# A transformer pair on one core: seven products for eight in half of the steps of four more turns, with the gt2 loads among them

## The reference

```
mod = silu(c) @ w_ada + b_ada                # 6 x 2048: sh1, sc1, gt1, sh2, sc2, gt2
...attention of the first block; x = x + gt1 * mix
h2  = rms_norm(x, g_norm2) * (1 + sc2) + sh2
ffn = (silu(h2 @ w_gate) * (h2 @ w_up)) @ w_down      # 2048 -> 5632 -> 2048
x   = x + gt2 * ffn
...second block: convolution, forgetting attention, gates, relu^2 feed-forward 2048 -> 8192 -> 2048
```

## Time and profile before

| | us |
|---|---|
| median of three runs | 2602.41 (2600.86 to 2602.66) |
| the profiled execution | 2601.97 |
| its span, first to last instruction | 2600.2 |
| TensorE busy | 2550.3 (98%) |
| VectorE busy | 1781.0 (68%) |
| ScalarE busy | 1258.8 (48%) |
| GpSimd busy | 55.2 (2%) |
| granted TensorE clock, mean | 0.995 |

### The profile page before, as it was taken

One profiled execution on the slowest core, in us unless ns is written; L12 is line 12 of the kernel. 1 busy time (PEld: TensorE's weight loads), 2 busy tenths in 40 slices (PEclk: granted clock), 3 DMA queues, 4 the chain that ended last, 5 costly groups with the idle time before them and its releaser, 6 DMA issues.

```text
span 2600.2 us, 31671 instructions
## 1 busy us (share of the span) xinstructions
PE 2550.3 (98%) x11970; PEld 2048.5 (79%) x11970; DVE 1781.0 (68%) x2059; ACT 1258.8 (48%) x1647; POOL 55.2 (2%) x88
## 2 busy tenths in 40 slices
PE   7999989999999999999999999999999999999998
PEld 3677757788888888888888888888888888888886
DVE  2356664767779998978655455556689778777855
ACT  2344554443444555544544455444456555455544
POOL 1010110000000000000000000000000000000000
PEclk9999999999999999999999999999999999999999
DMA  9968776757776555565655545656655565556563
GB/s 392 400 229 304 260 273 224 260 199 244 248 246 217 202 203 199 194 215 190 212 194 178 178 162 167 206 200 211 200 177 198 189 221 192 186 188 220 190 196 121
DMA packets 263722, 564.34 MB, mean 217 GB/s; under 512 B 9315, under 2 KB 13589, under 8 KB 262445
## 3 DMA queue, kind: packets, MB, share of 16 engines
q1 hardware_dynamic: 261264, 549.25, 61.1%
q0 software_dynamic: 1952, 11.27, 1.2%
q10 hardware_dynamic: 380, 2.13, 0.2%
HBM read 558.40 MB, written 4.21 MB: 216 GB/s over the span
## 4 chain that ended last, share of the span: by engine, by line
PE 84%; DVE 2%; ACT 1%; issue 0%; POOL 0%; DVEq 0%; ACTq 0%; POOLq 0%
PE acc L528 59%; PE acc L885 15%; PE bank L885 3%; PE bank L611 2%; PE acc L923 1%; PE bank L560 1%; DVE w_lo L1998 1%; PE acc L848 0%; PE acc L761 0%; PE acc L813 0%; PE bank L770 0%; PE acc L759 0%; PE bank L623 0%; PE acc L1071 0%; PE acc L1072 0%
## 5 line engine op out<-in xcount | busy, mean ns | idle before, releaser
L1998 DVE TENSOR_TENSOR w_lo<-raw,w_hi 128x1024 fp32r<-128x1024 f32 x852 | 1008.3, 1193 | 582.6 <-ACT w_hi L1375 552.1
L1375 ACT ACTIVATE w_hi<-raw 128x1024 fp32r<-128x1024 f32 x804 | 845.7, 1059 | 761.4 <-PE acc L528 581.8
L528 PE MATMUL acc<-w_hi,actT_hi 128*128 128x512 f32 (+1 forms) x1344 | 531.4, 395 | 2.6 <-DVE actT_lo L2149 1.6
L528 PE MATMUL acc<-w_hi,actT_lo 128*128 128x512 f32 (+1 forms) x1344 | 521.3, 388 | 0.0
L528 PE MATMUL acc<-w_lo,actT_hi 128*128 128x512 f32 (+1 forms) x1344 | 520.9, 388 | 0.0
L528 PE MATMUL acc<-w_hi,mixT_hi 128*128 128x512 f32 (+1 forms) x1256 | 494.9, 394 | 2.5 <-DVE mixT_lo L2138 2.1
L528 PE MATMUL acc<-w_hi,mixT_lo 128*128 128x512 f32 (+1 forms) x1256 | 488.5, 389 | 0.0
L528 PE MATMUL acc<-w_lo,mixT_hi 128*128 128x512 f32 (+1 forms) x1256 | 487.8, 388 | 0.0
L528 PEld LDWEIGHTS acc<-w_hi,actT_hi 128*128 128x128 f32 x1344 | 252.4, 188 | 78.1 <-issue 19.1
L528 PEld LDWEIGHTS acc<-w_hi,actT_lo 128*128 128x128 f32 x1344 | 252.3, 188 | 52.3
L528 PEld LDWEIGHTS acc<-w_lo,actT_hi 128*128 128x128 f32 x1344 | 252.6, 188 | 50.0 <-issue 1.1
(11 more groups left out here) (357 smaller groups left out, 2000.9 us busy)
## 6 DMA issues: line engine op xcount, KB each, us to landing
raw<-in_w_ff SPq DMA_DIRECT2D x128, 1024.0 KB, 5.2
raw<-in_w_in SPq DMA_DIRECT2D x108, 1024.0 KB, 5.1
raw<-in_w_ada SPq DMA_DIRECT2D x64, 1024.0 KB, 6.4
raw<-in_w_gate SPq DMA_DIRECT2D x44, 1024.0 KB, 5.1
raw<-in_w_up SPq DMA_DIRECT2D x44, 1024.0 KB, 5.7
raw<-in_w_down SPq DMA_DIRECT2D x44, 1024.0 KB, 5.2
early_mix<-in_w_ada SPq DMA_DIRECT2D x16, 1024.0 KB, 10.5
wide<-in_w_ada SPq DMA_DIRECT2D x16, 1024.0 KB, 8.7
```

Source lines behind the costliest of these rows:

```text
L528: last_mm = pe.matmul(acc[p][:, t, 0:width], act[x][:, k0 + c, t * P:(t + 1) * P], w[:, u % SPL, c * NW:c * NW + width], start=first and c ...
L1375: act.activation(w_hi[:, u % SPL, :], raw[:, ld % RAW, slot[2] * 1024:(slot[2] + 1) * 1024], ACT.Copy).then_inc(hi_ready, 1)
L1998: dve.tensor_tensor(w_lo[:, u % SPL, 0:n], src, w_hi[:, u % SPL, 0:n].bitcast(F32), ALU.subtract).then_inc(lo_ready, 1)
```

## The change

Two of the four steps of gate and up in turns 1 to 4 become seven-product steps; the other two stay as units. The four "a" loads of a turn are placed one load sooner (after the first to the fourth weight load instead of after the second to the fifth), so that they lie ahead of the pairs. VectorE's gt2 products move with them: the first of a turn falls into the last down group of the turn before, and for the first turn into the first gate and up block. The activation differences are written in that same block, after units 7, 9, 11 and 13. `wide` is cleared by GpSimd behind its load of the gt2 bias, and VectorE waits for that before its first hidden product. Three of the four turns are a loop on TensorE, ScalarE and VectorE; SP's loads of these turns are written out.

```diff
-ORDER += "w" * 8 + ("w" + "wa" * 4 + "w" * 7) * 4 + "w" * 12 * 6 + "w" * 4
+ORDER += "w" * 8 + ("wa" * 4 + "w" * 8) * 4 + "w" * 12 * 6 + "w" * 4
...
-S_LOADS = [len(GAPS) + 8 + 4 * 12 + 12 * t for t in range(S_TURNS)]
+F1_LOAD = len(GAPS) + 8
+S_LOADS = [F1_LOAD + 12 * t + 4 for t in range(4)]
+S_LOADS += [F1_LOAD + 4 * 12 + 12 * t for t in range(S_TURNS)]
...
-        for _ in range(S_STEPS):
+        for _ in range(S_STEPS if w >= F1_LOAD + 4 * 12 else S_STEPS // 2):
             slots_ += [("pair", w, 1, w + 1), ("sums", 1), ("sums", 0), ("quarter", w + 1, 3), ("half", w + 1, 0),
                        ("half", w, 0)]
+            events += [DU * w, DU * w + 1, DU * w + 2, DU * w + 3, None, None]
...
@@ TensorE
-            def strassen(mixes):
+            def strassen(mixes, plain=0):
...
+                def ends(ins):
+
+                    ins.then_inc(unit_used, 1)
+                    modulate()
+                for j in range(plain):
+                    for p in (0, 1):
+                        if j == 0:
+                            acc_taken(p)
+                        for h in range(DU):
+                            u = next_slot()
+                            for c in range(UC):
+                                for t in range(TT):
+                                    ins = product(acc[p][:, t, :], tok(4 * j + 2 * h + c, t), u, c,
+                                                  j == 0 and h == 0 and c == 0, False)
+                            ends(ins)
+                for j in range(plain, S_STEPS):
...
-            loop(3, {**turn_, "bank": 4, "groups": 1, "load": 16}, ffn1)
-            ffn1(None)
             pe.wait_ge(mixed_ready, S_STEPS)
...
+            loop(3, {"unit": S_SLOTS - 4, ("acc", 0): 1, ("acc", 1): 3, ("acc", 2): 3, "stg": 1, "bank": 6, "groups": 1},
+                 lambda i: ffn1s(i, S_STEPS // 2))
+            ffn1s(None, S_STEPS // 2)
...
@@ GpSimd
             pool.dma_start(grow, b_ada("gt2").partition_broadcast(P)).then_inc(gt2_bias, 16)
+            pool.memset(wide[:, :, :], 0.0).then_inc(wide_cleared, 1)
...
@@ VectorE
             units(16, {**{j: lambda j=j: split_tmp_to(ACTT, 2 * j + 4) for j in range(6)}, 8: gate_taken,
-                       9: lambda: link(dve.memset(wide[:, :, :], 0.0))})
+                       **{7 + 2 * j: lambda j=j: mix_pair(j, mixes1) for j in range(S_STEPS)}})
+            dve.wait_ge(wide_cleared, 1)
             hidden()
             hidden_lo()
...
-            units(16, {8: gate_taken, **{10 + 2 * j: lambda j=j: mix_pair(j, mixes1) for j in range(3)}})
...
-            def strassen():
-
-                at = 6 * S_STEPS
+            def strassen(plain=0):
+
+                at = 6 * S_STEPS - 2 * plain
                 units(at, {at - 5: second_sum, at - 4: third_sums, at - 2: up_sum, at - 1: gate_sum})
```

More of the change, by code:

```diff
@@ L914, in strassen @@
                     u = next_slot()
-                    ins = product(bank[b7][:, :], x7, u, 1, first, last)
+                    ins = product(bank[b7][:, :], x7, u, 1, opens, last)
                     if last:
                         ins.then_inc(bank_full[b7], 1)
-                    product(bank[b5][:, :], x5, u, 0, first, last).then_inc(unit_used, 1)
+                    ends(product(bank[b5][:, :], x5, u, 0, opens, last))
                     if first:
@@ L925, in strassen @@
                             ins.then_inc(bank_full[b5], 1)
-                    ins.then_inc(unit_used, 1)
+                    ends(ins)
                     for p in (1, 0):
@@ L955, in _, with ffn1s @@
             turn_stage()
[L957 to L964, removed]
-            loop(3, {**turn_, "bank": 4, "groups": 1, "load": 16}, ffn1)
-            ffn1(None)
             pe.wait_ge(mixed_ready, S_STEPS)
-            def ffn1s(i):
-                strassen(mixes1)
+            def ffn1s(i, plain=0):
+                strassen(mixes1, plain)
                 down(None, accs=(2, 1))
@@ L1280, in _ @@
             gate_up(0)
[L1282 to L1289, removed]
+            for block_ in range(1, 5 + S_TURNS):
                 for r in range(0, D, 4 * P):
@@ L1677, in _ @@
             hidden_hi()
[L1679 to L1682, removed]
-            turn_ = {"unit": 24, "split": 24, "stg": 1, "bank_hi": 2}
-            loop(3, {**turn_, "bank": 4, "load": 16}, ffn1)
-            ffn1(None)
             def save_first(read=True):
@@ L1697, in silu_sum, with ffn1s @@
                 act.activation(sq, sq, ACT.Silu).then_inc(act_ready, 1)
-            def ffn1s(i):
+            def ffn1s(i, plain=0):
                 skip_banks(2)
-                units(S_SLOTS, {6 * S_STEPS - 5: save_first, 6 * S_STEPS: silu_sum})
+                n = 6 * S_STEPS - 2 * plain
+                units(n + 8, {n - 5: save_first, n: silu_sum})
                 L.next("stg")
                 hidden_hi()
+            loop(3, {"unit": S_SLOTS - 4, "split": S_SLOTS - 4, "load": 16, "stg": 1, "bank_hi": 2, "bank": 6, "sums": 2,
+                     "gate": 1}, lambda i: ffn1s(i, S_STEPS // 2))
+            ffn1s(None, S_STEPS // 2)
             loop(S_TURNS - 1, {"unit": S_SLOTS, "split": S_SLOTS, "load": 12, "stg": 1, "bank_hi": 2, "bank": 4,
@@ L2636, in ffn1s @@
                 hidden_lo()
+            loop(3, {"unit": S_SLOTS - 4, "split": S_SLOTS - 4, "load": 16, "act": 1, "stg": 1, "bank_hi": 2, "bank": 6,
+                     "dch": 4 + 3 + 2 * 2 + 12 + 2, "first": 1, "gate": 1, "up": 1, "groups": 1},
+                 lambda i: ffn1s(i, S_STEPS // 2))
+            ffn1s(None, S_STEPS // 2)
             loop(S_TURNS - 1, {"unit": S_SLOTS, "split": S_SLOTS, "load": 12, "act": 1, "stg": 1, "bank_hi": 2, "bank": 4,
```

51 lines of the change are left out of this document (20 added, 31 removed).

## The result

The changed kernel takes 2608.70 us (median of 12 runs, 2606.10 to 2610.38) where the kernel before takes 2602.28 beside it (12 runs, 2600.83 to 2603.74): a ratio of 1.0026, 95% interval 1.0018 to 1.0034. That is 6.4 us slower, while the forecast was 2604.8, no change. The profiled run took 2608.38 us with a span of 2606.6, against 2601.97 and 2600.2 before.

What follows compares the result with a forecast made beforehand. TensorE was taken to set the time while VectorE delivers its splits in time. Terms -5.44 + 2.25 + 1.7 + 3.2 + 0.9 = +2.6 gave 2604.8 us, range 2598.5 to 2608.8.

Steps and rivals of the forecast that it cites:

- 24 matmuls: Turns one to four: seven-product steps issue 45 matmuls for 48, 24 fewer in all at 0.2267 us each, -5.44 us.
- hidden product late: End of the first gate and up block: differences and first gt2 product delay VectorE's hidden product, +2.25 us.
- clock behind it (first turn): After the first block: TensorE's idleness of about 3.6 us is followed by 1.2 GHz, +1.7 us.
- waits of turns two to four: Third slot of the first seven-product step: TensorE waits 1.2 us a turn for VectorE, +3.2 us in all.
- memset on GpSimd: Near 511.6 us: VectorE's cast at 514.21 waits for the memset's end at 515.1, +0.9 us.
- rivals 2 and 3: Around 512 us: a wait stretched by the memset also lowers the clock, 1.7 us more; 2606.4 (chance 0.12) and 2609.8 (0.13).
- Rival 3: Around 512 us: memset lasts 7 us, cast starts 4.4 us late and the clock falls; +7.8, 2609.8 us, chance 0.13.
- The queue walk: VectorE's work from a turn's third down group to the next turn's third slot: 32.7 us, making TensorE wait 1.2.
- Rival 1: Turns: VectorE keeps up, queue gaps close when it is behind, later turns lose nothing; 2598.8 to 2601.4 us, chance 0.25.
- The loads one place sooner: Turns' loads: landings stay hidden, the pair sums' load with 0.3 us to spare; cost 0, up to 1.8 a turn.
- nothing comes back: First block: removing VectorE's 3.47 us memset at 549.84 gains no time, as VectorE had caught up by 558.69.

## Why the prediction was wrong

Of +6.4 us the forecast had +2.6. Its terms against the trace, where the turns are taken against those of before (67.17, 67.08, 67.09, 67.12) less 1.36:

| term | forecast | measured |
|---|---|---|
| 24 matmuls | -5.44 | -5.44 (turn of 65.72 in the run with short gt2 products, 65.82 in that with fewer differences) |
| hidden product late | +2.25 | +2.26 |
| clock behind it (first turn) | +1.7 | +1.43 |
| waits of turns two to four | +3.2 | +3.40, of it 2.93 at the third slot and 0.29 at the slot before it in the fourth turn |
| memset on GpSimd | +0.9 | +4.57 |

These make +6.2; 0.5 us more lie ahead of 512 us, where three executions of one kernel (the one in pieces) lie up to 3.4 us apart, and 0.3 less past 900 us.

**The step that failed is "The memset on GpSimd".** Its start (511.6 forecast, 512.07 here, where all comes 0.5 later) and its length (3.5 forecast, 3.53) were right. Wrong was which VectorE instruction it meets: "If the cast waits for the memset's end, it starts 0.9 us late". I looked for what VectorE does when the memset *ends* and took the cast at 514.21. But GpSimd is itself the one that releases the diagonals: it makes rstd (done at 511.49), issues the bias load and goes on to the memset, and VectorE starts the first TENSOR_SCALAR 0.04 us after rstd. The instructions to look for are those that VectorE begins around the memset's *beginning*. Both were held for its whole length, with TensorE waiting for just that. By the rows before (0.57 us for both) the first would have been done ahead of 512.07, so it was held by something that GpSimd did before its memset's row begins; the same bias load alone held nothing before, and whether the bias load and the memset behind it hold VectorE together, the memset takes hold early or GpSimd's rows are only inexact, no run tells. Held until 520.87, the same memset costs TensorE nothing; in the kernel before, alone, it costs 4.8.

The Trainium skill ("SBUF — State Buffer", section "Who interferes with whom") says that whoever issues first has the shared ports for its whole instruction and that tensor_scalar counts among those that can want them. The trace agrees with the second half: TENSOR_SCALARs of 0.3 us ended behind the memset's 3.53, and beside pieces of 0.5 they grew by at most 0.3. The prediction's other half, that a memset does not hold a subtraction, shows as well: with the memset held, the split at 520.32 runs 0.67 us into it and keeps its 1.22, and beside the pieces a subtraction at 513.40 keeps its 0.69. With the first half the trace agrees only if the memset is issued before its row begins, for the TENSOR_SCALARs' rows begin first. I had the rule and applied it to the wrong row.

**The clock there** was a term that only rivals 2 and 3 had, at 1.7 us behind a wait that the memset stretches. It measured 1.58. Rival 3 came nearest in time (2609.8), but by a memset of 7 us that does not exist; its price was right for another reason, and that is no forecast.

**The queue walk** stood. Its places were right in all three turns and its size, 1.2 us forecast for 1.05 and 1.07, nearly so. The fourth turn loses less at that slot, 0.81, as said; but 0.29 goes at the slot before, behind the late load, which the walk did not have. That 3.2 forecast and 3.40 measured lie so close is in part luck. The first turn had no wait. Rival 1, that gaps close when VectorE is behind, is refuted. With no wait and no lower clock a turn of the changed kernel would take 66.84 - 1.05 = 65.79 us, the 65.7 of the forecast (65.72 where the queue is short).

**The loads one place sooner** were priced at nothing. In the change as made that nearly holds: only in the fourth turn is a load late, the one to which I gave "0.3 us to spare". It is issued at 789.02 and lands 5.9 us later, where I took 5.1, and VectorE waits 0.56 for it; every profiled version with this order of the loads and full gt2 products shows 0.4 to 0.9 us there. But there was more in it than I saw. I followed the load of the first pair and not that of the second, whose buffer changes its owner with the order: one place back costs 11.4 to 11.9 us a turn. And with the gt2 products cut to a quarter of their width VectorE waits 2.5 to 3.5 us for that same load in every turn. That "nothing comes back" for VectorE's memset held: with it gone 4.8 us were lost, and the wait and the clock at 512 account for 4.6 of them.

## What to carry to other kernels

Before work is put on GpSimd, read which VectorE instructions start around its start, half a microsecond ahead of it too, not only what runs at its end: in these runs a cast or TENSOR_SCALAR that a long memset met lasted to the memset's end. Where GpSimd itself releases VectorE, as here with rstd, the next long GpSimd instruction is likely to meet what was released; hold it by a semaphore until VectorE has slack. When a queue sets a wait, take work or a wait out of it rather than move work within it: of the edits here that moved work within the queue only one gained, which took a product out from ahead of the one that TensorE was waiting for.

## What the runs showed that was not expected

- The TENSOR_SCALARs' rows begin 0.54 and 0.3 us ahead of the memset that holds them.
- How long TensorE stays at 1.2 GHz after the same wait differs between kernels alike at that place: after 4.15 to 4.21 us of idleness the first unit's first matmul took 0.50 us in five profiled runs and 0.79 or 0.80 in two, with the granted clock still at 0.50.
- Waits of 3.57 or 3.58 us were followed by transposes of 1.97 (two runs), 1.70, 1.43, 1.41 and 1.09 us. With the order of the loads as changed the first turn then took 67.24 to 67.43 us each time, also behind the 1.09, where the lower clock came later. Of three waits of 2.17 or 2.18 us one was followed by it (the differences moved, alone); waits of 1.39 to 1.70 us at that place were not.
- The memset in eight pieces takes 4.11 us for 3.53, and its kernel's times fall into two groups some 8 us apart.
- A memset on GpSimd of 128x4096 took 3.51 to 3.53 us in every run, as long as VectorE's 3.47.
